# Sixteen small transfers per feed-forward block: three behind each weight slab in place of four, and the work around them moved

## The reference

```
for layer in range(2):
    xn = rmsnorm(h, tok_norm_g[layer])
    mix, q_mem = mixer(xn, ...)
    mo = memory_attention(q_mem, mem_n, mem_w_kv[layer])
    h = h + concatenate([mix, mo]) @ tok_w_out[layer]
    hn = rmsnorm(h, ffn_norm_g[layer])
    # ffn_w1 is 2048 x 8192, ffn_w2 is 8192 x 2048
    h = h + square(relu(hn @ ffn_w1[layer])) @ ffn_w2[layer]
return rmsnorm(h, final_norm_g)
```

## Time and profile before

| what | value |
|---|---|
| median of three runs | 2362.38 us |
| lowest and highest run | 2357.18 and 2366.48 us |
| the profiled execution's own time | 2364.97 us |
| its span, first to last instruction | 2363.0 us |
| TensorE matmul busy | 2292.9 us (97%) |
| VectorE busy | 1429.1 us (60%) |
| ScalarE busy | 1262.7 us (53%) |
| share of the 16 DMA engines, SP's queue | 61.3% |
| granted TensorE clock, mean | 0.995 |

### The profile page before, as it was taken

How to read it: one execution, slowest core, us unless ns; L and a number is a source line. 1 busy time by engine, 2 the same in 40 slices (tenths; PEclk the granted TensorE clock), 3 DMA queues, 4 the chain that set the end, 5 groups by cost and what they waited for, 6 DMA issues and landing times.

```text
span 2363.0 us, 32861 instructions
## 1 busy us (share of the span) xinstructions
PE 2292.9 (97%) x10629; PEld 1900.0 (80%) x10629; DVE 1429.1 (60%) x2449; ACT 1262.7 (53%) x2303; POOL 41.6 (2%) x58
## 2 busy tenths in 40 slices
PE   9999999999999999999999999999999999999998
PEld 7888888888877788877778888888777888777787
DVE  6678797796755555545555555556445555454555
ACT  6575565564555544445544555545455444454544
POOL 0010100000000000000000000000000000000000
PEclk9999999999999999999999999999999999999999
DMA  9655464553666666666666675666666666566665
GB/s 335 176 151 161 121 176 123 166 162 109 179 191 194 205 197 194 195 186 201 193 203 193 186 217 145 182 191 199 189 197 194 198 194 194 179 205 191 203 193 177
DMA packets 257130, 439.64 MB, mean 186 GB/s; under 512 B 36076, under 2 KB 54381, under 8 KB 256877
## 3 DMA queue, kind: packets, MB, share of 16 engines
q1 hardware_dynamic: 256285, 436.96, 61.3%
q10 hardware_dynamic: 720, 1.06, 0.1%
HBM read 419.00 MB, written 2.10 MB: 178 GB/s over the span
## 4 chain that ended last, share of the span: by engine, by line
PE 74%; SPq 12%; DVE 4%; DMA 3%; ACT 3%; issue 3%; POOL 0%; ACTq 0%; POOLq 0%; DVEq 0%
PE pair L572 23%; PE pair L574 22%; PE pair L573 22%; SPq L442 9%; SPq L397 3%; PE aux L765 3%; DMA xn_late<-xn_late 3%; PE aux L583 2%; DVE w_lo L1591 2%; ACT hid_hi L1462 1%; ACT w_hi L1063 1%; DVE r L1918 1%; PE aux L812 0%; DVE attnT L1912 0%; DVE projections L1818 0%
## 5 line engine op out<-in xcount | busy, mean ns | idle before, releaser
L1591 DVE TENSOR_TENSOR w_lo<-raw,w_hi 128x512 fp32r<-128x512 f32 x1536 | 1021.9, 691 | 806.0 <-ACT w_hi L1063 803.1
L1063 ACT ACTIVATE w_hi<-raw 128x512 fp32r<-128x512 f32 x1536 | 934.3, 631 | 730.4 <-DMA raw<-in_ffn_w 570.3
L572 PE MATMUL pair<-w_hi,xT 128*128 128x512 f32 x1984 | 789.3, 398 | 48.1 <-DVE w_lo L1591 46.6
L573 PE MATMUL pair<-w_lo,xT 128*128 128x512 f32 x1984 | 777.0, 392 | 0.0
L574 PE MATMUL pair<-w_hi,xT 128*128 128x512 f32 x1984 | 776.7, 391 | 0.0
L572 PEld LDWEIGHTS pair<-w_hi,xT 128*128 128x128 f32 x1984 | 374.7, 189 | 137.3 <-DVE w_lo L1591 57.8
L574 PEld LDWEIGHTS pair<-w_hi,xT 128*128 128x128 f32 x1984 | 375.0, 189 | 80.0
L573 PEld LDWEIGHTS pair<-w_lo,xT 128*128 128x128 f32 x1984 | 375.3, 189 | 74.4
L572 PE MATMUL pair<-w_hi,hid_hi 128*128 128x512 f32 x1012 | 395.0, 390 | 11.8 <-DVE w_lo L1591 11.8
L574 PE MATMUL pair<-w_hi,hid_lo 128*128 128x512 f32 x1012 | 393.9, 389 | 0.0
L573 PE MATMUL pair<-w_lo,hid_hi 128*128 128x512 f32 x1012 | 393.8, 389 | 0.0
(11 more groups left out here) (250 smaller groups left out, 1107.8 us busy)
## 6 DMA issues: line engine op xcount, KB each, us to landing
raw<-in_ffn_w SPq DMA_DIRECT2D x1024, 256.0 KB, 3.1
raw<-in_dn_w_in SPq DMA_DIRECT2D x208, 256.0 KB, 2.9
raw<-in_tok_w_out SPq DMA_DIRECT2D x128, 256.0 KB, 3.1
raw<-in_gm_w_in SPq DMA_DIRECT2D x112, 256.0 KB, 2.9
raw<-in_mem_w_kv SPq DMA_DIRECT2D x64, 256.0 KB, 3.3
xn_late<-xn_late SPq DMA_DIRECT2D x512, 32.0 KB, 2.3
r<-in_mem_columns SPq DMA_DIRECT2D x8, 256.0 KB, 5.2
h<-in_x_columns SPq DMA_DIRECT2D x8, 256.0 KB, 5.8
```

The lines of the kernel that those rows point to most:

```text
L572: pe.matmul(acc, act_hi[:, kt, tokens], w_hi[:, slot], start=start, stop=False)
L573: pe.matmul(acc, act_hi[:, kt, tokens], w_lo[:, slot], start=False, stop=False)
L1063: act.activation(w_hi[:, slot], raw[:, slot], ACT.Copy).then_inc(hi_ready, 1)
L1591: dve.tensor_tensor(w_lo[:, slot], raw[:, slot], w_hi[:, slot].bitcast(F32), ALU.subtract).then_inc(tiles_split, 1)
```

## The change

SP issues three of the sixteen transfers behind each of the loads of slabs 2 to 6, and the sixteenth alone behind slab 7. The squares of ScalarE go from behind split 4 to behind split 3, and its high parts from behind split 3 to behind split 5. VectorE's transposes go from behind splits 5 and 6 to behind splits 4 and 5. The low parts stay in the code where they are, behind split 4, with their wait for the high parts; within `s == 4` they stand ahead of the transpose.

```diff
                     with sp.Fori(0, 3) as it:
                         for j in range(2):
                             for s in up(it * 2 + (2 + j)):
-                                if 1 <= s < 5:
-                                    move_hidden(block_of(layer, half, j) + it * 2, half, j, s - 1)
+                                if 2 <= s:
+                                    move_hidden(block_of(layer, half, j) + it * 2, half, j, s - 2)
                     for s in down(0):
-                        if 1 <= s % 8 < 5:
-                            move_hidden(block_of(layer, half, 6 + s // 8), half, s // 8, s % 8 - 1)
+                        if 2 <= s % 8:
+                            move_hidden(block_of(layer, half, 6 + s // 8), half, s // 8, s % 8 - 2)
...
-                a = part
...
-                for b in range(4):
-                    dst, src = moved[32 * a:32 * a + 32, b], turned[32 * b:32 * b + 32, a]
-                    sp.dma_start(dst, src).then_inc(sem(f"hidden_moved{half}{j}"), 16)
+                for square in range(3 * part, min(3 * part + 3, 16)):
+                    a, b = square // 4, square % 4
+                    sp.dma_start(moved[32 * a:32 * a + 32, b], turned[32 * b:32 * b + 32, a]).then_inc(sem(f"hidden_moved{half}{j}"), 16)
...
-                    if s == 3 and before is not None:
+                    if s == 5 and before is not None:
                         it, j = before
                         act.wait_ge(sem(f"hidden_moved{half}{j}"), it * 256 + (1024 * layer + 256))
...
-                    if s == 4 and last is not None:
+                    if s == 3 and last is not None:
                         it, j = last
...
-                    if s in (5, 6) and last is not None:
+                    if s in (4, 5) and last is not None:
                         it, j = last
-                        m = s - 5
+                        m = s - 4
```

## The result

The changed kernel takes 2561.36 us (median of 4 runs, 2557.3 to 2562.33) against 2359.78 us for the kernel before on the same chip: ratio 1.0847, 95% interval 1.0818 to 1.0876. It is 8.5% slower, 201.6 us. The forecast was 2500 us with a range up to 2545. The sign and the place were right, the size was too small.

The account below looks back on a forecast made before the run. TensorE was taken as the bound, stalling once in each of 32 blocks with moves. Stall 95.8 plus clock 41.6 gave 137.4 us on the profiled 2364.97: 2502.4, carried to the median about 2500 us, range 2448 to 2545.

Parts of the forecast that it names:

- The transpose's 0.62 us: VectorE, in front of split 5: the first transpose adds 0.62 us to the stall, in 28 blocks.
- while the moves end 5.01 us later: SP's queue: the sixteenth move starts at 702.80, before 697.79; less 2.72 us, this gives 2.29 us more stall.
- The tail: From hid_hi's start to TensorE's restart: 3.23 us in place of 2.45, 0.78 more; 0.16 more in each half's last block.
- stall term: TensorE before slab 5 in 32 blocks: 95.8 us more stall in all, mean stall 4.8 us in place of 1.77.
- clock term: Slow TensorE clock after all 32 stalls: 51.2 us, less 9.6 already paid, so 41.6 us more.
- Eight such matmuls cost 8 x 0.20 = 1.6 us: TensorE after a stall: eight matmuls at the 1.2 GHz level, 0.433 us apart in place of 0.2266, cost 1.6 us.
- Rival (c): TensorE's clock: two slow stretches after each stall, 92.8 us, so 2551 us; chance 0.09.
- (b): TensorE: the stall comes but the clock stays, 2458 us; chance 0.09.
- (d): SP's queue: SP doesn't fall behind with three moves a slab, 2450 us; chance 0.11.
- (f): Whole kernel: time stays within 0.5% because another slack, such as faster landings, gives it all back; chance 0.03.
- (e): VectorE: low parts do not hold up slab 5, only slab 6 waits; 14 us less, 2348 us; chance 0.02.
- An edit costed at nothing: ScalarE's squares and VectorE's second transpose, one slab sooner, lie in idle time: 0 us; uncovered, squares are 1.1 us per block.

Follow-up runs that it names:

- fifth experiment: The changed kernel with VectorE's transposes back behind splits 5 and 6: 2536.69 us.
- second: The changed kernel with the sixteen moves dealt 3, 3, 3, 3, 4 over slabs 2 to 6, none behind load 7: 2467.52 us.
- eighth: The changed kernel with the sixteen moves dealt 3, 3, 2, 2, 2, 4 over loads 2 to 7: 2526.49 us.
- seventh kernel: The changed kernel with low parts behind split 6, three moves a slab behind loads 1 to 5 and the sixteenth behind load 6: 2300.46 us.
- first experiment: The changed kernel with VectorE's low parts behind split 6 in place of split 4: 2399.89 us.
- fourth: The kernel before with only ScalarE's and VectorE's parts of the change, SP's moves as before: 2411.57 us.
- third: The kernel before with only SP's part of the change; squares, transposes, high and low parts as before: 2607.75 us.
- sixth: The kernel before with ScalarE's and VectorE's parts of the change, and low parts behind split 6: 2301.40 us.
- ninth: The kernel before with high parts behind split 5 and low parts behind split 6, all else as before: 2339.68 us.
- tenth: The seventh kernel with squares and transposes at their old places, behind splits 4, 5 and 6: 2342.47 us.

## Why the prediction was right or wrong

**Right, and shown.** The place and cause: VectorE's untouched wait under `s == 4` stops slab 5, and putting it behind split 6 alone takes away 161 us. SP's pace of 3.03 us a slab is in the trace to the hundredth. The position of the lone move, 0.45 us ahead of the time at which slab 5 is due: it was 768.28 - 767.90 = 0.38 us. The transpose's 0.62 us: 15.4 us measured for 28 blocks by the fifth experiment against 17.4.

**Wrong, first: the landing of the sixteenth move.** The step is "while the moves end 5.01 us later". It took the difference of the two issue times for that of the landings, and so carried 1.83 us over silently. The move had changed its neighbour: before it was the fourth behind a load (2.2 us), now the only one (0.39 us). It landed in 2.79 us, 0.96 later; the second and eighth experiments set that back to 1.83 and 1.84 by putting other moves between. Over 32 blocks this is 31 us; by the mean landing on the chain in all 32 blocks of each trace, 1.97 and 2.89 us, it is 29.5 us. The tail was 3.34 us in place of 3.23, 3.5 us in all, and the move's position another 0.07 us, 2 us in all. These terms, read from one block, come to 35 to 37 us against a miss of the stall term of 33 us: 185.6 - 56.6 = 129.0 us measured, 95.8 forecast.

The trace of the kernel before held this price. The move at 688.70, the first behind load 3b and 0.39 us behind it, took

```profile
DMA to landing us min/median/max: 2.5/2.5/2.5
```

(tile xn_late, window 688.6 to 688.8), and not 1.83. Instead I had the earlier trace rows with its 3.7 us in hand, and used it as a bound for the weight loads, which it does not describe: their own median is 3.1 us.

The Trainium skill, page "DMA: Bandwidth & Descriptors", section "Queues, rings and completion order", says that each DMA engine consumes a queue's descriptors in ring order. A move right behind a load of 256 KB then has that load's pieces ahead of it. The trace agrees: 2.79 us at 0.39 us behind a load, 0.18 us after that load's own landing, and 1.84 at 2.21.

**Wrong, second: the size of the clock term.** The step is "Eight such matmuls cost 8 x 0.20 = 1.6 us", taken for each stall. That all 32 stalls would be followed by slow matmuls was right. But the block shown has 14 slow intervals, 2.9 us. To price this for each kernel, I take its span less its stalls, less the same of the seventh kernel (2298.6 - 8.1 = 2290.5 us, 8.1 being its waits outside the start of the program), less 0.17 us a stall, because a stop is counted from the end of a matmul that lasts 0.39 us and not from the next start at 0.23:

| kernel | mean stall, us | span less stalls, us | clock cost, us | slow stretches | us each |
|---|---|---|---|---|---|
| before | 1.77 | 2306.4 | 10.5 | 6 | 1.7 |
| first | 2.51 | 2317.0 | 21 | 13 | 1.6 |
| fourth | 2.73 | 2323.7 | 28 | 17 | 1.6 |
| second | 3.61 | 2344.5 | 49 | 29 | 1.7 |
| eighth | 5.06 | 2359.9 | 64 | 32 | 2.0 |
| fifth | 5.32 | 2363.9 | 68 | 32 | 2.1 |
| changed | 5.80 | 2374.8 | 79 | 32 | 2.5 |
| third | 7.70 | 2359.8 | 64 | 32 | 2.0 |

The slow stretches are counted in the trace's record of the granted clock. The term of 1.6 us was right for mean stalls up to 3.6 us and too small above. The forecast had 41.6 us over before, measured are 79 - 10.5 = 68 us: 27 short. Rival (c) put this term at 92.8 us, 24 too many. That its 2551 us lies 10 us from the measured time is luck, since its stall term is 33 us short.

Where the price comes from can be read in the same record. What costs is the part of a slow stretch that lies behind the restart; each us of it loses 1 - 0.2266 / 0.433 = 0.48 us. That part is 3.4 us in the mean in the kernel before and in the first, fourth and second, 4.3 in the eighth, 4.5 in the fifth, 5.3 in the changed and 4.3 in the third: 1.6, 2.0, 2.1, 2.5 and 2.0 us, the last column of the table. In the third kernel the clock falls 3.6 us ahead of the restart in the mean, in the changed one 1.1 us, so much of the third's slow time passes while TensorE stands. Its block of above, with the restart at 776.52:

```profile
772.52:776.52 4.00, 0.00 (x1) 0.00 (x1) 0.75 (x2) 2.45 (x5) 0.00 (x0) 0.51 0.16 59
776.52:780.52 4.00, 4.00 (x12) 3.22 (x13) 4.00 (x7) 3.91 (x8) 0.00 (x0) 0.64 0.00 0
```

Both misses have the same sign: 95.8 + 41.6 = 137.4 us forecast, 129.0 + 68.4 = 197.4 us by the two profiles (201.6 by the medians).

**The other rivals.** (b) and (d) are out: the clock fell each time, and SP did fall behind. (f) is out too: the time moved. (e), the low parts not holding up slab 5, was not what the changed kernel does, but the first experiment built it: 2400 us and not 2348, because its price also carried the 1.83 us landing and hardly any clock.

**An edit costed at nothing.** The sooner squares and transposes were rightly taken as hidden in the changed kernel: SP doesn't wait for them there. The margin behind them was not kept as a price: once the stall is gone it is worth 38 us (sixth against ninth) and 42 us (seventh against tenth).

## What to carry to other kernels

When one of a pair of dependent steps is moved on one engine, look at its partner on the next: with in-order engines a consumer left at its old place stops all the weight work behind it, and here moving that line too took back 161 of 202 us. Such savings don't add: with SP's moves put back instead it was 150. A transfer's landing time belongs to its place in the queue, so price a moved transfer by a row with the same neighbour in front. And price a long stall with its own slow matmuls: a row from a 2.4 us stall is too small for one of 5.8, since more of the slow stretch then lies behind the restart.

## What the runs showed of the hardware

- A 32 KB transfer within SBUF mostly lands in 1.83 to 1.89 us when issued 2.2 us behind a 256 KB load. Issued 0.39 us behind one, as the lone move of the changed kernel, it lands 0.16 to 0.22 us after that load: 2.6 to 2.9 us in the 24 up blocks, 3.2 to 3.65 us in the eight down blocks.
- What a slow stretch of the clock costs does not simply grow with the stall: 1.6 to 1.7 us with mean stalls of 1.8 to 3.6 us, 2.5 at 5.8 us, and 2.0 at 7.7 us. It goes with the slow time behind the restart, 3.4, 5.3 and 4.3 us in the mean.
- Stalls between 1.8 and 3.3 us were followed by a slow stretch in some blocks and not in others: 6 of 32 stalls in the kernel before, 13 of 32 in the first experiment, 17 of 32 in the fourth. No shorter stall of these twelve kernels was, and every longer one was.
